# Two of the three branch products as seven half-size products per 1024 columns, with weight sums formed from HBM to HBM

## The reference

```python
h = layer_norm(x, ln_in_g, ln_in_b)                       # (512, 2048)
proj = h @ w_in                                           # queries, keys, values, gates of A, B, C and mg
branches = (oa * silu(ag), ob * silu(bg), oc * silu(cg))  # three attentions, each (512, 1024)
for n in range(3):
    gate = sigmoid(mg[:, n * 2048:(n + 1) * 2048] + b_gate[n])
    merged += gate * (branches[n] @ w_branch[n])          # (512, 1024) @ (1024, 2048)
h = layer_norm(alpha * h + merged @ w_out, ln_g, ln_b)    # (512, 2048) @ (2048, 2048)
```

## Time and profile before

| | us |
|---|---|
| median of 3 runs (1840.96 to 1842.37) | 1841.87 |
| the profiled execution, its own time | 1840.76 |
| its span in the profile | 1838.9 |
| PE busy | 1822.7 (99%) |
| DVE busy | 1317.2 (72%) |
| ACT busy | 863.3 (47%) |

### The profile page before, as it was taken

How to read it: one execution, slowest core, us unless ns; L and a number is a source line. 1 busy time by engine, 2 the same in 40 slices (tenths; PEclk the granted TensorE clock), 3 DMA queues, 4 the chain that set the end, 5 groups by cost and what they waited for, 6 DMA issues and landing times.

```text
span 1838.9 us, 24157 instructions
## 1 busy us (share of the span) xinstructions
PE 1822.7 (99%) x8577; PEld 1513.7 (82%) x8577; DVE 1317.2 (72%) x2086; ACT 863.3 (47%) x1458; POOL 201.9 (11%) x276
## 2 busy tenths in 40 slices
PE   9999999999999999999999999999999999999997
PEld 7888888888888888888888888888888888888885
DVE  5777764887777775566678878878788645566778
ACT  5653332545555554344445555555456333244643
POOL 1111110100212120000000000000001000002222
PEclk9999999999999999999999999999999999999998
DMA  9576676962643433444263451624527544439987
GB/s 330 182 206 177 186 198 214 237 218 66 178 122 94 117 101 110 118 116 140 69 193 106 170 189 53 217 69 161 201 75 285 184 149 149 149 115 238 245 211 176
DMA packets 226470, 299.38 MB, mean 163 GB/s; under 512 B 13585, under 2 KB 140625, under 8 KB 224337
## 3 DMA queue, kind: packets, MB, share of 16 engines
q1 hardware_dynamic: 171824, 188.24, 32.2%
q0 software_dynamic: 54416, 109.51, 22.2%
q10 hardware_dynamic: 144, 0.52, 0.1%
HBM read 247.73 MB, written 50.97 MB: 162 GB/s over the span
## 4 chain that ended last, share of the span: by engine, by line
PE 97%; DVE 1%; DMA 1%; ACT 0%; issue 0%; DVEq 0%; POOL 0%; POOLq 0%; SPq 0%; ACTq 0%
PE acc L668 10%; PE acc L670 10%; PE acc L669 10%; PE scores L863 6%; PE scores L861 6%; PE scores L859 6%; PE acc L863 3%; PE acc L861 3%; PE acc L859 3%; PE transposed L693 3%; PE scores L1104 2%; PE scores L1102 2%; PE scores L1103 2%; PE attended L863 2%; PE attended L861 2%; PE attended L859 2%
## 5 line engine op out<-in xcount | busy, mean ns | idle before, releaser
L1292 ACT ACTIVATE piece_split<-w 128x512 fp32r<-128x512 f32 x448 | 282.9, 633 | 288.4 <-PE scores L863 105.1
L1854 DVE TENSOR_TENSOR piece_split<-w,piece_split 128x512 fp32r<-128x512 f32 x448 | 309.1, 691 | 110.2 <-ACT piece_split L1292 98.5
L1708 DVE TENSOR_TENSOR w_lo<-raw_weights,w_hi 128x1024 fp32r<-128x1024 f32 x181 | 220.3, 1220 | 179.0 <-ACT w_hi L1187 177.7
L668 PE MATMUL acc<-h_hi,w_lo 128*128 128x512 f32 x800 | 319.3, 399 | 0.0
L670 PE MATMUL acc<-h_hi,w_hi 128*128 128x512 f32 x800 | 312.4, 391 | 0.0
L669 PE MATMUL acc<-h_lo,w_hi 128*128 128x512 f32 x800 | 311.7, 390 | 0.0
L1187 ACT ACTIVATE w_hi<-raw_weights 128x1024 fp32r<-128x1024 f32 x181 | 191.2, 1060 | 190.3 <-PE acc L1104 52.2
L670 PEld LDWEIGHTS acc<-h_hi,w_hi 128*128 128x128 f32 x800 | 150.2, 188 | 32.4
L668 PEld LDWEIGHTS acc<-h_hi,w_lo 128*128 128x128 f32 x800 | 150.4, 188 | 29.8 <-issue 1.8
L669 PEld LDWEIGHTS acc<-h_lo,w_hi 128*128 128x128 f32 x800 | 150.6, 188 | 28.5
L859 PE MATMUL scores<-piece_split,h_lo 128*128 128x512 f32 x384 | 149.6, 390 | 0.0
(11 more groups left out here) (447 smaller groups left out, 3675.3 us busy)
## 6 DMA issues: line engine op xcount, KB each, us to landing
w<-in_w_in SPq DMA_DIRECT2D x128, 512.0 KB, 7.4
raw_weights<-in_w_in SPq DMA_DIRECT2D x102, 512.0 KB, 3.9
raw_weights<-in_w_branch SPq DMA_DIRECT2D x48, 512.0 KB, 5.2
raw_weights<-in_w_mem_kv SPq DMA_DIRECT2D x32, 512.0 KB, 5.4
gate<-gate_scratch POOLq DMA_DIRECT2D x12, 1024.0 KB, 6.6
h_sums<-sums_scratch POOLq DMA_DIRECT2D x6, 1024.0 KB, 10.4
gate_scratch<-first_product POOLq DMA_DIRECT2D x12, 512.0 KB, 6.3
out_w_x<-in_w_out POOLq DMA_DIRECT2D x12, 512.0 KB, 8.4
```

The lines of the kernel that those rows point to most:

```text
L668: pe.matmul(bank_out, wl, hi[:, k, :], start=first, stop=False)
L1292: act.activation(p_split[:, n % RING, 0, :], sources[p][:, k, :], ACT.Copy).then_inc(pc_hi, 1)
L1708: dve.tensor_tensor(w_lo[:, slot, :], raw[:, slot, :], w_hi[:, slot, :].bitcast(F32), ALU.subtract).then_inc(lo_ready, 1)
L1854: dve.tensor_tensor(p_split[:, n % RING, 1, :], sources[p][:, k, :], p_split[:, n % RING, 0, :].bitcast(F32), ALU.subtract).then_inc(pc_lo, 1)
```

## The change

Branches C and B are no longer multiplied plainly. For each of them and each 1024 columns (a *set*, s = 0 to 3: C, C, B, B) there are seven products of half size (quarters of 4 row blocks, 2 token tiles, 512 columns), in the order of the gate groups. A product has two chunks, a chunk 12 matmuls. Branch A stays plain and comes last, in four steps.

- The sums of weight quarters (T1 to T4 of every set, 1 MB each) are made by DMA alone: 32 transfers of 1 MB on POOL's queue from HBM to HBM, in 24 slots, one at the start of the products G5, G6, G2 and G7 of each of the six gate groups. 16 of them are plain copies ("set"), 16 add into their target. Each slot waits until all earlier ones have landed. SP waits for all 32 before it loads the first chunk.
- The sums of the branches' quarters are made by DVE (`halved_sum`, 128 x 1024 each), for C in gate group 7, for B in sets 0 and 1. Three of them come at a time when the products still go on.
- The bias of the gates is written into `gate_dram` beforehand (12 transfers of 1 MB, HBM to HBM, in the stages of B and A), and `store_gate` now adds into it. `gate_rows` and the 12 loads of the bias are gone.
- Set s leaves its products in `p1_buf`, `p5_buf` and `u2_buf`, as the gate groups do; DVE adds the banks to them and multiplies by the gates. Merged rows now have a tile of their own per 512 columns, and `fill_merged` comes once in each of the steps 1 to 3 of branch A.
- At the junction ACT splits the first three chunks and the first two left tiles between the pieces of the last product, and before it copies set 0's first product it waits until all four stores of the gates have landed.
- Buffers of the output stage move to other addresses; its order of products stays.

The diff, cut to its core:

```diff
+HALVED = 4
+ALL = GROUPS + HALVED
+STEPS = 2 * PRODUCTS
...
+T_PLAN = [[("set", T1, (0, 0)), ("set", T3, (0, 1))], [("add", T1, (0, 1))],
+          [("add", T3, (1, 1)), ("set", T2, (1, 1))], [("add", T2, T1)], [("set", T4, (1, 0))], [("add", T4, T2)]]
...
@@ SP
             sp.wait_ge(t_ready, t_index(GROUPS, 1, 0))
-            for m in range(N_BRANCH * (D // 512)):
...
+            sp.wait_ge(toep_stored, TOEP_DONE + 16 * 8 * HALVED)
+            for s in range(HALVED):
+                for p in range(PRODUCTS):
+                    src = t_dram[s, RIGHT[p]] if p in (G5, G6, G7, G4) else branch_weights(2 - s // 2, s % 2, RIGHT[p])
+                    for h in range(2):
+                        c = CH_M + STEPS * s + 2 * p + h
+                        load(c, c % RING, src[2 * h * P:2 * (h + 1) * P, :].rearrange("(k p) n -> p k n", p=P), 2)
...
@@ PE
+            def halved_product(s, p, banks, first, stop):
...
+                if s % 2 == 0:
+                    pe.wait_ge(branch_ready, PRODUCTS * (s // 2) + p + 1)
+                for h in range(2):
+                    c = CH_M + STEPS * s + 2 * p + h
+                    pe.wait_ge(lo_ready, c + 1)
+                    for kk in range(2):
...
+                        for t in range(2):
+                            tok = slice(t * P, (t + 1) * P)
+                            pe.matmul(banks[t][:, :], lo[:, k, tok], wh, start=first and k == 0, stop=False,
...
+                            pe.matmul(banks[t][:, :], hi[:, k, tok], wl, start=False, stop=False,
...
+                            last = pe.matmul(banks[t][:, :], hi[:, k, tok], wh, start=False,
...
+                pe.wait_ge(ev_c11, 2 * g)
+                halved_product(s, G1, z, True, False)
+                pe.wait_ge(ev_c12, 2 * g + 2)
+                halved_product(s, G5, y, True, False)
+                pe.wait_ge(ev_s1, 2 * g + 2)
+                halved_product(s, G6, z, False, False)
+                pe.wait_ge(ev_c21, 2 * g + 2)
+                halved_product(s, G2, x, True, True)
+                pe.wait_ge(ev_u2, 2 * g + 2)
+                halved_product(s, G7, z, False, False)
+                pe.wait_ge(ev_s5, 2 * g + 2)
+                halved_product(s, G3, y, False, True)
+                pe.wait_ge(ev_c22, 2 * g + 2)
+                halved_product(s, G4, z, False, True)
...
@@ ACT, gate group 7
-                        if g == GROUPS - 1 and p in (G3, G4) and k % 2:
-                            branch_hi(2, k // 2 + (4 if p == G4 else 0))
+                        if g == GROUPS - 1 and p == G4 and k in (3, 5, 7):
+                            split_hi_now(CH_M + k // 2 - 1)
+                        if g == GROUPS - 1 and p == G4 and k in (4, 6):
+                            halved_hi(0, k // 2 - 2)
...
@@ ACT, sets
+            for s in range(HALVED):
+                z, y, x = gate_banks(GROUPS + s)
+                for j in range(STEPS):
+                    split_hi(CH_M + STEPS * s + j)
+                    if s == 0 and j < 4:
+                        halved_hi(0, G2 + j)
+                    if s == 0 and j == 2:
+                        for done in (st_c11, st_c22, st_c12, st_c21):
+                            act.wait_ge(done, 16 * GROUPS)
+                    if j == 2:
+                        copy_halved(s, 2, z, p1_buf, ev_s1, 2)
...
@@ DVE, gate group 7
+                        if g == GROUPS - 1 and (p, k) in ((G2, 5), (G2, 7), (G7, 2), (G7, 4), (G7, 6)):
+                            halved_sum(0, (k - 5) // 2 if p == G2 else k // 2 + 1)
...
@@ DVE, sets
+                    split_lo(CH_M + STEPS * s + j)
...
+                    if j == 10:
+                        job_done(CH_M + STEPS * s + 9)
+                        dve.wait_ge(ev_s5, 2 * g + 2)
+                        add_out(z, p5_buf, ev_c22)
...
+                    if s == 0 and j in (5, 6, 7):
+                        halved_sum(1, j - 5)
...
@@ POOL
-                pool.dma_start(dst.rearrange("t p n -> p t n"), buf[:, :, :]).then_inc(done, 16)
+                    pool.dma_start(dst.rearrange("t p n -> p t n"), buf[:, :, :], accum_op=ALU.add).then_inc(done, 16)
+
+            def weight_sums(slot):
+
+                s, n = slot // len(T_PLAN), slot % len(T_PLAN)
+                before = 8 * s + sum(len(ops) for ops in T_PLAN[:n])
+                if slot:
+                    pool.wait_ge(toep_stored, TOEP_DONE + 16 * before)
+                for kind, dst, src in T_PLAN[n]:
+                    rows = t_dram[s, src] if src in (T1, T2) else branch_weights(2 - s // 2, s % 2, src)
...
             def store_group(g):
+                if g >= KV_GROUPS:
+                    for n, p in enumerate((G5, G6, G2, G7)):
+                        pool.wait_ge(pc_mult, piece(g, p, 0))
+                        if g == GROUPS - 1 and p == G6:
+                            load_branch(2, br_raw[0][:, :, :])
+                        weight_sums(4 * (g - KV_GROUPS) + n)
...
             load_gate(1)
-            load_branch(0, h_lo_raw[:, BT:KT, :])
+            load_branch(1, br_raw[1][:, :, :])
```

More of the change, by code:

```diff
@@ L1085, in _ @@
+            pe.wait_ge(ev_c11, 2 * ALL)
+            pe.wait_ge(ev_c12, 2 * ALL + 2)
+            for m in range(D // 512):
                 for s in range(4):
-                    c = CH_M + 4 * m + s
+                    c = CH_PLAIN + 4 * m + s
                     pe.wait_ge(lo_ready, c + 1)
@@ L1561, in _ @@
                 gate_group(g)
-            for n in range(LOOKAHEAD):
-                split_hi_now(CH_M + n)
+            halved_hi(0, G6)
             copy_c21(GROUPS - 1)
@@ L2270, in _ @@
                 gate_group(g)
[L2271 to L2289 removed]
+            split_lo_now(CH_M + 2)
@@ new lines, in halved_21 @@
+            def halved_21(s):
+                z, nb = gate_banks(GROUPS + s)[0], 2 * (s % 2)
+                job_done(CH_M + STEPS * (s + 1) - 1)
+                for t in range(2):
+                    gate_times(z[t][:, :], 0, 2 + t, 1.0, (sums[nb] if s < 2 else gate[0])[:, 2 + t, :]).then_inc(ev_c21, 1)
+                if s >= 2:
+                    for t in range(2):
+                        dve.wait_ge(ev_c21, 2 * (GROUPS + s) + 2 + t + 1)
+                        dve.tensor_tensor(sums[nb][:, 2 + t, :], sums[nb][:, 2 + t, :], gate[0][:, 2 + t, :],
+                                          ALU.add).then_inc(m_sum, 1)
@@ L2712, in load_v, with preset_gates @@
                         .then_inc(v_loaded, 16)
+            def preset_gates(k):
+                n, nb = k // 4, k % 4
+                rows = gate_dram[n, nb].rearrange("t p n -> (t p) n")
+                pool.dma_start(rows, b_gate[0][n, nb * 512:(nb + 1) * 512].partition_broadcast(SEQ))\
+                    .then_inc(preset, 16)
             for done in (st_c11, st_c22, st_c21):
```

446 lines of the change are left out of this document (294 added, 152 removed).

## The result

The changed kernel takes 1850.52 us (median of 4 runs, 1848.39 to 1851.29), the kernel before 1841.41 on the same chip: a ratio of 1.0049, interval 1.0037 to 1.0061. It is slower by 9 us where 10.6 less were forecast; 1850.52 also lies outside the range of 1821 to 1843. The profiled execution took 1850.94 us, with a span of 1849.1.

A forecast was written before the change was run, and what follows sets the result against it. PE was taken as the bound, busy 1822.7 of 1838.9 us. 1840.8 - 21.8 + 2 + 4.7 + 1 + 2.5 + 1 = 1830.2 us, with 1.1 more for the median 1831; range 1821 to 1843.

The forecast's parts named there:

- The saving: Branch stage: 1152 matmuls become 1056; 96 x 0.227 = 21.8 us saved on PE.
- The step that failed: Weight-sum slots in gate groups before group 7: 10.9 us each, a rest of 43, nobody waits; no cost.
- the bias preset: 12 plain MB in POOL's queue, one per head pair, where PE waits for nothing: 0, at most 3 us.
- The chain of sums in group 7: Gate group 7: slot 23 lands at +53, SP's chunks begin at +62.8; 10 us early, cost 0.
- rival B: HBM-to-HBM sums come too late, SP begins 22 us late: 1851 us; decides at 12.4 us per add; 9%.
- The end of gate group 7: Last product: ACT's split of chunk 0 delays piece 4, then DVE's work: 2 us, bounds 0 and 4.
- Set 0's first copy: ACT's copy waits for quarter 21's store, landing after 12.3 us; PE stands 4.7 us, bounds 0.4 and 10.4.
- Branch B: Set 0: B's 2 MB load takes 24 us, DVE stands some 7 us: 2.5 us, bounds 0 and 8.
- The sets' DVE: All four sets: DVE's work fits, 35.2 of 38.1 us in set 0; fifth product's add late: 1 us, bounds 0 and 8.
- rival C: Sets bound by DVE or by the DMA engines all along, 2 us stop per set: about 1840, end 1843.8; 13%.
- The clock: After set 0's first-copy stop: a stop of over 2 us puts PE to 1.2 GHz; 1 us, bounds 0 and 5.4.
- The output stage: One sum of merged rows moves behind the last step, where DVE idles: 0, at most 2 us.

The follow-up runs named there:

- add_before_split: Changed kernel, with DVE adding the fifth product ahead of the split at j = 10 in every set: 1849.82 us, ratio 1.0052.
- store_wait_later: Changed kernel, with ACT's wait for the four gate stores in set 0 moved from j = 2 to j = 6: 1849.41 us, ratio 1.0047.
- copies_first: fixed_front, with ACT copying a finished product before splitting the next chunk and waiting for the stores at j = 6 of set 0: 1836.49 us, ratio 0.9973.
- branch_a_halves: Changed kernel, with set 2's gates loaded first, then branch A in two 1 MB transfers three chunks apart, its tiles split later: 1851.30 us, ratio 1.0055.
- sets_spread: copies_first plus add_before_split's edit, branches B and A each loaded in two spread halves, B's sums and A's tiles later: 1831.27 us, ratio 0.9943.
- fixed_front: Changed kernel with both moves: bias presets 8 to 11 into branch B's pairs, weight-sum slots 0 to 3 into branch A's: 1836.85 us, ratio 0.9980.
- no_bias: Changed kernel with the gate bias left out (no presets of the gates, plain gate stores): 1834.34 us, ratio 0.9957.
- sums_out_of_group2: Changed kernel, with weight-sum slots 0 to 3 issued in pairs 1 to 4 of branch A instead of gate group 2: 1842.26 us, ratio 1.0005.
- merged_sum_first: Changed kernel, with DVE making the output stage's third merged-row sum ahead of the second weight double's split: 1851.95 us, ratio 1.0057.

## Why the prediction was wrong

- **The saving.** 96 x 0.227 = 21.8 us: right. The last column of the table stays within 2 us of 1819.0 whatever the stops were.
- **The step that failed** is "The earlier groups have 10.9 us per slot and a rest of 43 us, and nobody waits for them", together with the bias preset at "0, at most 3". I took PE's empty list of waits for slack. It says that the loads came in time, not by how much. Around the starts of groups 2 and 3 the DMA engines were busy 0.77 and 0.82 of the time already in the kernel before, and I had looked at group 7 alone, at its idle middle (0.00). 12.8 us came from there, with a term of 0 and an upper end of 3. Both moves together take it back, 13.7 us. Part of the step is POOL's queue: I counted 10.9 us per slot from the product's start, and in group 2 POOL came to slot 0 at 969.8, behind the last store of branch A, and to slot 3 some 14 us after its product had begun.
- **The chain of sums in group 7.** Right. The group begins at 1328.3 + 12.8 = 1341.1. Slot 23 was issued at 1386.13 (+45, forecast +44), and with the 8.6 us of an add of T onto T it landed at about +54, where +53 was forecast. SP's first chunk went out at 1402.75, +61.7, where it had been +62.8 in the kernel before. The longest of the 16 adds took 11.7 us, below the 12.4 at which rival B decides:

```profile
DMA to landing us min/median/max: 7.9/10.1/11.7
```

  (L2912, the adds.) The 16 plain copies in the same slots read 6.1/9.9/14.5. By the Trainium skill (Collectives: The Full Stack, "Why ReduceScatter is half of AllGather", which speaks of the adding step of a collective) an add would be 11.4 us by estimate. The 10.1 measured lies below it, and twice the time of a copy is not to be seen: 10.1 stands beside 9.9. One detail was wrong without effect: slot 21 does not wait for branch C's load to land, it was issued at +26.
- **The end of gate group 7.** 1.1 us, predicted 2.
- **Set 0's first copy.** The stop is there, at the place named and released as named (ACT's copy after 5.1 us of waiting for `gate_scratch<-first_product`): 3.2 us for 4.7. The store landed in 11.1 us where I had taken 12.3. That they add cost the stores about 2 to 3 us each (medians of 9.1, 5.8 and 9.1 us for the three buffers, 6.3, 3.4 and 7.2 before), where I had taken 3.
- **Branch B.** 2.0 us for 2.5. The load took 21.8 us for 24, and DVE stood for it as said, for 4.3 us instead of 7 (waits from 1417 to 1458):

```profile
DVE branch_sums L2153 <- DMA branch_unsplit<-branch_scratch: 4.3, 1, 4.3
```

  How much of the 2.0 is the load's isn't separated: add_before_split left 0.5 of it with the load as it was.
- **The sets' DVE**, 1 us, bounds 0 and 8: mis-sized. The stops behind it came to 8.4 us (1.4, 0.7, 3.7, 1.0, 1.2, 0.4), just outside its upper end. I had counted DVE's busy time (35 of 38 us; measured 31 to 33 in each set), but what is late is a chunk. In set 2, 2 MB of branch A and 2 MB of gates go out within 8 us beside chunks that want 193 GB/s. The four chunks straight from `w_branch` that are issued from 1490 to 1530 land in 9.3 us as a median (the eight from the sums in 4.0), and ACT, whose copy PE waits for, stands in front of its split (1505 to 1532):

```profile
ACT w_hi L1273 <- DMA raw_weights<-in_w_branch: 8.5, 2, 5.5
```

  Changes of order alone on ACT or DVE passed most of it on (store_wait_later, add_before_split, copies_first), and so did halves alone (branch_a_halves); order and halves together took 6 us of it away (sets_spread against fixed_front). That comes nearest to rival C's second half, "by the DMA engines", which I let the first half hide; but it holds in bursts and not all along, since over each whole set the share was 0.71 to 0.85.
- **The clock**, 1 us for the stop at set 0's first copy: mis-sized too, and misplaced. After that stop (2.9 us of waiting) the clock read 1.00 and cost nothing, while 2.7 us after each of the two stops at the front and 1.9 in set 2 were lost at the lower level. The sentence "a stop of over 2 us puts PE to 1.2 GHz", taken from one place at the kernel's end, does not hold: see the last section.
- **The output stage**, 0, at most 2: 4.8 us, so this zero was wrong too. The sum of the third merged rows stands on DVE ahead of the last adds, and a transfer of `out_w_x` is late. In the experiments the first could be removed alone, the second could not.

Predicted stops 11.2 us, measured 32.3: 1830.2 + 21.1 = 1851.3, beside 1850.94 profiled. The direction came out wrong by these 21 us, 12.8 of them from two places where the prediction did not look. Rival B's time (1851) was met by chance, by another mechanism than B's.

What stays open: how much of the output stage's second stop is due to which transfer, which of its edits sets_spread owes its gain to, and what decides whether the clock falls after a stop.

## What to carry to other kernels

A transfer that nobody waits for can still cost if it is in flight when a load starts for which somebody will. Before pricing it at nothing, read the DMA share in every window through which it passes, above all where each stage loads its first weights, and not only in the middle of a stage or where the changed code stands. A share near 1 does not by itself mean a stop (fixed_front read 1.07 and had none); it says where the landing of the next stage's first load has to be looked at. And find the time at which an in-order queue really comes to it. Where a fix passes the stop to the next wait, the wait's name is not its cause: look for what lands last.

## What the runs showed of the hardware

- **Slow presets.** 1 MB of the gate bias (rows of 2 KB, each written 512 times, from HBM to HBM) took 13.6 us as a median of 12, while 1 MB of `out<-in_ln_b` (rows of 8 KB) took 6.1. While the two presets ran, the window of the changed kernel read

```profile
936.00:944.00 8.00, 8.00 (x37) 6.61 (x36) 6.68 (x25) 4.86 (x20) 0.00 (x0) 1.00 0.96 147
```

  0.96 of the DMA engines for 147 GB/s, against 346 at 0.97 in the earlier trace rows. A share near 1 is thus not a rate. That the size of the rows is the reason wasn't tested.
- **Adding stores.** 512 KB from SBUF into `gate_scratch` in HBM took, by buffer, 6.3, 3.4 and 7.2 us to land as plain stores (medians, kernel before) and 9.1, 5.8 and 9.1 as adding ones (changed kernel). With plain stores again (no_bias) it took 6.7, 3.4 and 7.5.
- **The clock after a stop.** After PE's wait of 3.7 us at 958 the granted clock read 0.55 from 958 to 964. In sums_out_of_group2, after a longest wait of 3.0 us at the same place, it read 1.00:

```profile
958.00:964.00 6.00, 5.16 (x21) 3.62 (x21) 5.88 (x12) 2.45 (x5) 0.00 (x0) 1.00 0.96 285
```

  The length of PE's wait does not sort these cases. In the changed kernel the clock stayed at 1.00 behind the wait of 2.9 us in set 0 (first row) and fell behind the one of 1.9 us in set 2 (second row):

```profile
1432.00:1438.00 6.00, 5.49 (x24) 4.56 (x25) 4.56 (x5) 5.22 (x7) 0.00 (x0) 1.00 1.03 391
1526.00:1530.00 4.00, 4.00 (x11) 3.12 (x12) 1.78 (x3) 4.00 (x4) 0.00 (x0) 0.58 0.74 248
```

  At the stop in group 2, a wait of 3.3 us left it at 1.00 in add_before_split and one of 2.6 us was followed by 0.72 in merged_sum_first. The prediction had no row for a release in the middle of a kernel; these show one. PE's matmuls came every 0.43 us for some 3 to 6 us and then every 0.227 again, which cost 1.6 to 3.1 us beside the wait itself, each time that the clock fell.
